# First block's attention on one core: scores in two rounded passes over stacked keys, masks and maxima in rounded operands

## The reference, cut to what matters

```python
def window_attention(q, k, v, kc, vc, sink):
    ...
    s_loc = jnp.einsum('bnqkgd,bnjkd->bnkgqj', qb, kw).astype(jnp.float32) * scale
    s_ctx = jnp.einsum('bnqkgd,bckd->bnkgqc', qb, kc).astype(jnp.float32) * scale
    ...
    valid = (kpos >= 0) & (kpos < s) & (jnp.abs(qpos - kpos) <= WINDOW)
    s_loc = jnp.where(valid[None, :, None, None], s_loc, -jnp.inf)
    ...
    p = jax.nn.softmax(jnp.concatenate([s_loc, s_ctx, sl], axis=-1), axis=-1)

def global_attention(q, k, v, kc, vc):
    ...
    kall = jnp.concatenate([k, kc], axis=1)
    ...
    o = lax.map(lambda qblk: gqa_attend(qblk, kall, vall), qb)
```

## Time and profile before

| what | value |
|---|---|
| median of 3 runs | 3219.28 us (3214.47 to 3220.64) |
| the profiled execution, span from first to last instruction | 3215.5 us (its own time is not listed apart) |
| PE busy | 2983.4 us, 93% of the span |
| PE weight loads | 1880.8 us, 58% |
| DVE busy | 1100.8 us, 34% |
| ACT busy | 737.7 us, 23% |
| POOL busy | 381.7 us, 12% |
| mean granted clock of PE | 0.961 |
| first attention, 281.33 to 450.81 us | 169.5 us |
| second attention, 1272.23 to 1397.71 us | 125.5 us |

### The profile page before, as it was taken

One profiled execution on the slowest core, in us unless ns is written; L12 is line 12 of the kernel. 1 busy time (PEld: TensorE's weight loads), 2 busy tenths in 40 slices (PEclk: granted clock), 3 DMA queues, 4 the chain that ended last, 5 costly groups with the idle time before them and its releaser, 6 DMA issues.

```text
span 3215.5 us, 50344 instructions
## 1 busy us (share of the span) xinstructions
PE 2983.4 (93%) x21802; PEld 1880.8 (58%) x21802; DVE 1100.8 (34%) x1930; ACT 737.7 (23%) x1393; POOL 381.7 (12%) x494
## 2 busy tenths in 40 slices
PE   6999989699999998986988888999999999999999
PEld 3645556455555464554433333888865568678887
DVE  4124754211111244643222224322434463232242
ACT  3113651000000133541000002222322362222232
POOL 2022520122222121411000000000000000000000
PEclk8998989799999999997999999999999989999999
DMA  8930033899999810037999996122311202231130
GB/s 342 394 129 1 1 144 120 344 401 409 408 409 408 308 55 1 1 138 290 417 423 423 424 423 252 59 105 79 113 67 55 69 18 79 79 111 65 66 140 30
DMA packets 138400, 626.97 MB, mean 195 GB/s; under 512 B 12592, under 2 KB 19776, under 8 KB 82896
## 3 DMA queue, kind: packets, MB, share of 16 engines
q1 hardware_dynamic: 122064, 577.67, 44.8%
q0 software_dynamic: 16128, 46.18, 4.3%
HBM read 607.36 MB, written 16.45 MB: 194 GB/s over the span
## 4 chain that ended last, share of the span: by engine, by line
PE 42%; DMA 10%; DVE 2%; ACT 1%; issue 1%; SPq 0%; POOL 0%; DVEq 0%; ACTq 0%; POOLq 0%
PE bank L959 19%; DMA slots<-in_w_up_dram 10%; PE bank L1526 7%; PE bank L1714 4%; PE bank L1403 3%; PE bank L1630 3%; PE bank L1283 1%; PE bank L1647 1%; PE bank L1424 1%; PE bank L1658 0%; PE bank L1453 0%; PE bank L1648 0%; SPq L910 0%; PE bank L1060 0%; PE bank L1061 0%
## 5 line engine op out<-in xcount | busy, mean ns | idle before, releaser
L1403 PE MATMUL bank<-slots,HT 128*32 128x256 f32 x8192 | 478.0, 383 | 52.4 <-DMA slots<-in_w_gate_dram 24.2
L1403 PEld LDWEIGHTS bank<-slots,HT 128*32 128x32 f32 x8192 | 265.6, 111 | 269.0 <-issue 62.6
L959 PE MATMUL bank<-hT_high,chunk_high 128*128 128x512 f32 (+2 forms) x736 | 285.1, 387 | 5.3 <-DVE hT_low L2500 5.3
L959 PE MATMUL bank<-hT_high,low_slots 128*128 128x512 f32 (+2 forms) x736 | 287.1, 390 | 0.0
L959 PE MATMUL bank<-hT_low,chunk_high 128*128 128x512 f32 (+2 forms) x736 | 285.5, 388 | 0.0
L2091 ACT ACTIVATE arena<-bank 128x512 f32<-128x512 f32 x32 | 19.1, 597 | 756.2 <-PE bank L1403 433.8
L959 PE MATMUL bank<-slots,HT 128*128 128x512 f32 (+4 forms) x544 | 180.3, 491 | 7.2 <-issue 5.8
L2843 DVE TENSOR_TENSOR arena<-bank,arena 128x512 f32<-128x512 f32 x32 | 22.1, 692 | 441.9 <-ACT arena L2091 441.9
L959 PEld LDWEIGHTS bank<-hT_high,chunk_high 128*128 128x128 f32 x736 | 139.0, 189 | 35.7 <-DVE hT_low L2500 5.7
L959 PEld LDWEIGHTS bank<-hT_low,chunk_high 128*128 128x128 f32 x736 | 138.8, 189 | 32.4 <-issue 0.2
L959 PEld LDWEIGHTS bank<-hT_high,low_slots 128*128 128x128 f32 x736 | 138.7, 188 | 29.7
(11 more groups left out here) (453 smaller groups left out, 4897.4 us busy)
## 6 DMA issues: line engine op xcount, KB each, us to landing
slots<-in_w_gate_dram SPq DMA_DIRECT2D x128, 1024.0 KB, 19.5
slots<-in_w_up_dram SPq DMA_DIRECT2D x128, 1024.0 KB, 21.7
arena<-in_w_down_dram SPq DMA_DIRECT2D x80, 1024.0 KB, 23.3
arena<-in_ada_w_dram SPq DMA_DIRECT2D x48, 1024.0 KB, 9.1
X<-in_w_down_dram SPq DMA_DIRECT2D x32, 1024.0 KB, 18.3
slots<-in_w_in_dram SPq DMA_DIRECT2D x15, 2048.0 KB, 8.9
slots<-in_ffn_w_gate_dram SPq DMA_DIRECT2D x10, 2048.0 KB, 8.5
slots<-in_ffn_w_up_dram SPq DMA_DIRECT2D x10, 2048.0 KB, 8.9
```

Of the source, the lines that this page charges most:

```text
L959: mm = pe.matmul(out_, lhsT, rhs, start=(n == 0), stop=(n == len(pairs) - 1))
L1403: mm = pe.matmul(bank[32 * j:32 * j + 32, 2 + n, 256 * g:256 * g + 256], xT[:, 64 * k + 32 * g:64 * k + 32 * g + 32], columns(w[:, c, :], ...
```

## The change

It does the following, in both layers unless said.

- Keys are split into a rounded part and the rest. ACT rounds them into `k_high` (64 rows and the row of ones); DVE subtracts, writes the rest into partitions 64 to 127 of `k_both`, and copies the rounded part into partitions 0 to 63 (`stack_keys`). `k_both` lies on the place of `K_ext`.
- Queries are rounded by ACT into partitions 0 to 63 and once more into 64 to 127 of `q_twice` (for the first layer's context queries `q_twice_ctx`, which lies on the context tiles of `X`). POOL subtracts and keeps the rest of the queries in `q_low`, on the place of `Q_ext` (`query_rest`); row 64 there holds the negated maxima.
- A score product is `k_both` times `q_twice` over 128 rows, plus `k_high` times `q_low` over 65 rows: two rounded matmuls in place of a plain one.
- Row scores lose row 64, and the context groups' go through rounded operands too. The maxima that are subtracted are rounded (`neg_max`).
- The mask products use `mask_ident` and `mask_band`, rounded once by ACT in the first layer's `qkv`; the two copies that `latent_in` made of them go.
- ACT rounds the third and fourth main group at steps 1 and 3 of group 0; before, at step 1 of the first two main groups.
- The two context tiles of `X` are loaded in `conv_out` and no longer in `qkv`; POOL's memset of row 64 of the queries goes.

```diff
-        k_round = [rounded(f"k_round{l}", slots_at, unit % SLOTS * SLOT, 2, 2, NTOK) for l, unit in enumerate(first_slots("qkv"))]
-        q_round = [rounded(f"q_round{l}", slots_at, (unit + 1) % SLOTS * SLOT, 2, HEADS, SEQ)
+        k_high = [rounded(f"k_high{l}", slots_at, unit % SLOTS * SLOT, 2, 2, NTOK) for l, unit in enumerate(first_slots("qkv"))]
+        k_both = rounded("k_both", arena_at, at_moe, 2, 2, NTOK)
+        q_twice = [rounded(f"q_twice{l}", slots_at, (unit + 1) % SLOTS * SLOT, 2, HEADS, SEQ)
                    for l, unit in enumerate(first_slots("qkv"))]
+        q_twice_ctx = rounded("q_twice_ctx", X_at, ST * D, 2, HEADS, CTX)
+        q_low = [rounded(f"q_low{l}", slots_at, unit % SLOTS * SLOT, 2, HEADS, NTOK) for l, unit in enumerate(first_slots("w_out"))]
...
+        neg_max = nc.alloc_sbuf_tensor_at("neg_max", [P, 16], F32R, offset=neg_max_at)
...
+        mask_ident = nc.alloc_sbuf_tensor_at("mask_ident", [P, P], F32R, offset=mask_ident_at)
+        mask_band = nc.alloc_sbuf_tensor_at("mask_band", [P, 2, P], F32R, offset=band_at)
...
-                        mains = sum(other.main for other in groups[:group.number + 1])
-                        pe.wait_ge(sem["rounded"], st.at("rounded", 2 * mains))
+                        pe.wait_ge(sem["rounded"], st.at("rounded", (4 if st.layer == 0 else 3) * mains_to(group) - 1))
...
-                    kT = K_ext[0:HD + 1, group.kind, group.g, :]
+                    kT = k_high[st.layer][0:HD, group.kind, group.g, :]
                     if not group.main:
                         for j in range(2):
-                            mm = pe.matmul(bank[:, b, CTX * j:CTX * j + CTX], q_ext[0:HD + 1, group.kind, group.heads + j, tile_cols(qt)],
+                            mm = pe.matmul(bank[:, b, CTX * j:CTX * j + CTX],
+                                           q_twice_ctx[0:HD, group.kind, group.heads + j, tile_cols(qt - ST)],
                                            kT[:, SEQ:NTOK], start=True, stop=True)
                         mm.then_inc(sem["rowmax_full"], 1)
                         return
-                    kT = k_round[st.layer][0:HD + 1, group.kind, group.g, :]
-                    q = q_round[st.layer][0:HD + 1, group.kind, group.heads + unit.j, tile_cols(qt)]
...
                         pe.wait_ge(sem["shift_done"], st.at("shift_done", group.number + 1))
-                    keys = K_ext[0:HD + 1, group.kind, group.g, tile_cols(one.kt)]
+                        for name in ("rows_high", "rows_split") if group.main else ():
+                            pe.wait_ge(sem[name], st.at(name, mains_to(group)))
+                    both = k_both[:, group.kind, group.g, tile_cols(one.kt)]
+                    high = k_high[st.layer][0:HD + 1, group.kind, group.g, tile_cols(one.kt)]
+                    rest = q_low[st.layer][0:HD + 1, group.kind, :, :]
                     for j, b, event, previous in one.parts:
                         if previous is not None:
                             pe.wait_ge(sem["prob_ready"], st.at("prob_ready", previous + 1))
                         if j is None:
-                            pe.matmul(bank[:, b, :].rearrange("p (a n) -> p a n", a=2), keys,
-                                      q_ext[0:HD + 1, group.kind, group.heads:group.heads + 2, SEQ:NTOK],
-                                      start=True, stop=True).then_inc(sem["score_full"], 1)
+                            out_ = bank[:, b, :].rearrange("p (a n) -> p a n", a=2)
+                            pe.matmul(out_, both, q_twice_ctx[:, group.kind, group.heads:group.heads + 2, :], start=True, stop=False)
+                            pe.matmul(out_, high, rest[:, group.heads:group.heads + 2, SEQ:NTOK],
+                                      start=False, stop=True).then_inc(sem["score_full"], 1)
                             continue
                         edges = []
                         if group.kind == 0 and one.kt < ST:
                             edges = [(t, 0 if t < one.kt else 1) for t in (one.kt - 1, one.kt + 1) if 0 <= t < ST]
-                        mm = pe.matmul(bank[:, b, 0:one.hi - one.lo], keys, q_ext[0:HD + 1, group.kind, group.heads + j, one.lo:one.hi],
-                                       start=True, stop=not edges)
+                        pe.matmul(bank[:, b, 0:one.hi - one.lo], both, q_twice[st.layer][:, group.kind, group.heads + j, one.lo:one.hi],
+                                  start=True, stop=False)
+                        mm = pe.matmul(bank[:, b, 0:one.hi - one.lo], high, rest[:, group.heads + j, one.lo:one.hi],
+                                       start=False, stop=not edges)
                         for t, side in edges:
                             lo = P * t - one.lo
-                            mm = pe.matmul(bank[:, b, lo:lo + P], ident[:, :], band[:, side, :], start=False, stop=t == edges[-1][0])
+                            mm = pe.matmul(bank[:, b, lo:lo + P], mask_ident[:, :], mask_band[:, side, :], start=False, stop=t == edges[-1][0])
                         mm.then_inc(sem["score_full"], 1)
 
...
-                    act.activation(q_ext[HD:HD + 1, group.kind, group.heads:group.heads + 2, group.queries[0]:group.queries[1]],
+                    act.activation(q_low[st.layer][HD:HD + 1, group.kind, group.heads:group.heads + 2, group.queries[0]:group.queries[1]],
                                    bank[0:1, 4:6, 0:n], ACT.Copy).then_inc(sem["shift_done"], 1)
 
                 def round_operands(group):
 
                     kind, g = group.kind, group.g
-                    act.activation(k_round[st.layer][0:HD + 1, kind, g, :], K_ext[0:HD + 1, kind, g, :], ACT.Copy)                       .then_inc(sem["rounded"], 1)
-                    act.activation(q_round[st.layer][0:HD + 1, kind, 2 * g:2 * g + 2, :], q_ext[0:HD + 1, kind, 2 * g:2 * g + 2, 0:SEQ],
-                                   ACT.Copy).then_inc(sem["rounded"], 1)
+                    heads = q_ext[0:HD, kind, 2 * g:2 * g + 2, :]
+                    q = q_twice[st.layer][:, kind, 2 * g:2 * g + 2, :]
+                    q_ctx = q_twice_ctx[:, kind, 2 * g:2 * g + 2, :]
+                    act.activation(k_high[st.layer][0:HD + 1, kind, g, :], K_ext[0:HD + 1, kind, g, :], ACT.Copy).then_inc(sem["rounded"], 1)
+                    act.activation(q[0:HD], heads[:, :, 0:SEQ], ACT.Copy).then_inc(sem["rounded"], 1)
+                    if st.layer == 0:
+                        act.activation(q_ctx[0:HD], heads[:, :, SEQ:NTOK], ACT.Copy).then_inc(sem["rounded"], 1)
+                    doubled = act.activation(q[HD:P], heads[:, :, 0:SEQ], ACT.Copy)
+                    if st.layer == 0:
+                        doubled = act.activation(q_ctx[HD:P], heads[:, :, SEQ:NTOK], ACT.Copy)
+                    doubled.then_inc(sem["rounded"], 1)
...
-                        if n == 1 and to_round and group.main:
+                        if n in (1, 3) and to_round:
                             round_operands(to_round.pop(0))
...
+                def stack_keys(group):
+
+                    mains = sum(other.main for other in groups[:group.number + 1])
+                    dve.wait_ge(sem["rounded"], st.at("rounded", (4 if l == 0 else 3) * (mains - 1) + 1))
+                    keys, high, both = [v[:, group.kind, group.g, :] for v in (K_ext, k_high[l], k_both)]
+                    step(dve.tensor_tensor(both[HD:P], keys[0:HD], high[0:HD].bitcast(F32), ALU.subtract))
+                    dve.tensor_copy(both[0:HD], high[0:HD].bitcast(F32)).then_inc(sem["rows_high"], 1)
 
...
+                    if group.main:
+                        stack_keys(group)
                     for unit in group.units:
                         maximum(unit)
                 for group in groups:
                     units = groups[group.number + ahead].units if group.number + ahead < len(groups) else []
+                    if units and units[0].group.main:
+                        stack_keys(units[0].group)
                     for unit in units:
                         maximum(unit)
...
+                def query_rest(number):
+
+                    kind, heads = mains[number].kind, slice(mains[number].heads, mains[number].heads + 2)
+                    pool.wait_ge(sem["rounded"], st.at("rounded", (4 if l == 0 else 3) * (number + 1)))
+                    rest, whole = q_low[l][0:HD, kind, heads, :], Q_ext(l)[0:HD, kind, heads, :]
+                    ins = pool.tensor_tensor(rest[:, :, 0:SEQ], whole[:, :, 0:SEQ], q_twice[l][0:HD, kind, heads, :].bitcast(F32), ALU.subtract)
+                    if l == 0:
+                        ins = pool.tensor_tensor(rest[:, :, SEQ:NTOK], whole[:, :, SEQ:NTOK], q_twice_ctx[0:HD, kind, heads, :].bitcast(F32),
+                                                 ALU.subtract)
+                    ins.then_inc(sem["rows_split"], 1)
+
+                query_rest(0)
                 for part, (lo, hi) in enumerate(parts):
```

(8 more changed lines are left out.)

32 lines of the change are left out of this document (19 added, 13 removed).

## The result

The changed kernel took **3249.91 us** (median of 4 runs, 3241.33 to 3271.55), the kernel before 3217.07 in the runs beside it: a ratio of 1.011, 95% interval 1.0082 to 1.0138. It is 33 us slower, and 40 above the range's upper end. The profiled execution took 3257.27 us, with a span of 3255.4.

The account below looks back on a forecast made before the run. PE was taken to bound only cold and PE-bound pieces, with DVE and ACT holding the relays around group changes. First attention −14.2, second −14.3, loads +1 gave −27.5 us against the median 3219.28: 3192 us, range 3177 to 3210.

Parts of the forecast that it names:

- What PE gets back: Both attentions: PE work saved on scores, row scores and masks, 54.6 us at 2.4 GHz, a bound from above when warm.
- A score matmul becomes two rounded passes: Score products in both attentions: two rounded passes instead of four, so half of each matmul's time goes.
- 96 fewer mask records: Sign expected in the changed profile: mask products keep one record of two, so 96 go.
- The masks' 10.3 us saving: Mask products on PE: 96 records of 128 columns go, at about 0.107 us each, 10.3 us.
- POOL's first tap: First attention, group 0: ready at about 325 to 328 us, ACT stalls before its fifth tap, +3.5 us.
- the stacking: Key stacking ahead of DVE's maximum: +1.5 at 323 to 341, +0.7 at 358 to 379, +1.5 at 1337 to 1349.
- Rival (d): Both attentions: a less busy engine is granted 1.2 GHz longer; 60 us more there gives 33 slower, 3252 us; chance 0.05.
- Rival (b): Both attentions: relays hold nearly everything, only three PE-bound pieces give (12.3 us); gain 5, 3214 us; chance 0.15.
- Rival (c): Taps in group 0: DVE and POOL block each other wholly, 8 us worse, 3204 us; chance 0.10.
- third to a half: Overlap of DVE and POOL: priced as a slowing by this much, not as one blocking the other wholly.
- The loads at +1: Two x loads moved behind attention, ahead of six others on POOL's queue: later landing priced +1 us, between 0 and 2.5.
- the signs named as wrong: An attention over 20 us shorter, POOL's tap before ACT asks for the fifth, or cold stretches over 27.1 and 22.7 us.

Follow-up runs that it names:

- e8: The kernel before with sequence scores in two rounded passes and rounded masks, remainders left out, row scores over 65 partitions: 3194.05 us, ratio 0.992.
- e9: e5 without the remainders: DVE's key stacking left out, POOL's subtractions replaced by a zero fill, first score pass on the rounded keys: 3189.33 us, ratio 0.9923.
- e5: The changed kernel with its row-score matmuls over 65 partitions again instead of 64: 3222.94 us, ratio 1.0014.
- e7: The kernel before with its row-score matmuls of sequence queries over 64 partitions instead of 65: 3241.04 us, ratio 1.0072.
- e12: e5 without DVE's key stacking, so the keys' remainders stay out of the scores; POOL's query subtractions kept: 3202.79 us, ratio 0.9964.
- e13: e5 with POOL's query subtractions replaced by a zero fill, DVE's key stacking kept: 3202.86 us, ratio 0.997.
- e2: The kernel before with sequence score matmuls as two rounded passes instead of four, remainders left out, no work added on other engines: 3187.98 us, ratio 0.9907.
- e10: e8 with one rounded pass for each sequence score instead of two: 3184.21 us, ratio 0.9898.
- e1: The changed kernel with the first of its two rounded score passes issued three times, giving PE its old score load: 3256.9 us, ratio 1.0128.

## Why the prediction was wrong

The stages' way from 309.4 to 357.9 us, in measured steps: PE's passes and masks −27.6 (e8); ACT's further roundings, a fill on POOL, the later start and the rounded context scores +4.4 (e9); the remainders +30.3 (e5); 64 partitions +41.4. By the ratios of the whole times the same four are −26, +1, +29 and +31.

- **"What PE gets back"** was sound: 54.6 us at 2.4 GHz as a bound. e8 leaves the context queries as they were (3.4 + 5.1 of it), so 46 us of work went, PE's busy time fell by 36.8 and the stages by 27.6. "A score matmul becomes two rounded passes" and "96 fewer mask records" came true.
- **The step that failed** is one that isn't in the sum: the row scores went from 65 to 64 partitions and I priced that at nothing, without a sentence. It cost 41 us in the traces (31 by whole times): 29 (23) as gaps alone, as e7 has them at an unchanged clock, and the rest with the remainders around, where the changed kernel has 55 us more at 1.2 GHz than e5. The rest is near the scatter, and how it splits into waits and clock is open. The masks' 10.3 us saving turned into a loss by the price of 0.16 us: the 48 row masks now have a gap on either side, an estimated 15 us; the 48 masks of the score products stand beside 65 partitions and have none.
- **Mis-sized:** the side work. The sum had terms of 3.5 for POOL's first tap, 1.5 and 0.7 for the stacking in the first attention and 1.5 in the second, about 7 in all; the remainders cost 30. Each place was right: PE waited 4.5 us for the first roundings (4.0 before), the tap came at 327.01 us (predicted 325 to 328), ACT waited for it, `stack_keys` stood ahead of the maximum. But PE waited 7.7 us, not 3.5, and the stacking took up to 3.4 us beside POOL, not 1.5 to 1.9. Of the 30 us between e9 and e5, 19.8 are idle time of PE and 10.5 busy time, with 30 us more at 1.2 GHz. In the traces the larger part comes only when both parts are there, with 27 to 30 us of cold time (e5 against e12, e13), but the whole times have 13 and 15 us for each alone; which it is stays open.
- **Rival (d)**, slower by the clock, gave 3252, near the result, and for the most part for a wrong reason. Its premise, an engine with less to do, fails in e2 and e8, which keep the clock (69 and 77 us cold against 74). Its size was near: 104 us more at 1.2 GHz hold at most 52 us of full-clock work, where (d) had 60. But the clock fell with the gaps and the waits together; e7 has the gaps and e12 and e13 one source of waits each, and they have 73, 93 and 96 us cold against 178. Where exactly the grant turns stays open.
- **Rival (b)**, the relays hold, shows in e10, where PE idles for most of what it is spared. Rival (c), DVE and POOL blocking each other: stacking beside POOL took 3.4 us against 1.5 alone. The subtraction and the copy each took 0.95 us longer, twice and 2.7 times their time, beside POOL operations of 1.0 to 1.8 us. That is nearer to the whole blocking of (c) than to the "third to a half" that I took, but it was not tried by itself.
- The loads at +1: the stages behind the first attention up to the end of the output projection took 109.1 us before and 109.5 after.
- Of the signs named as wrong one did show: three cold stretches of 31 us, against 27.1 and 22.7, and 103 and 75 us cold in all. The other two did not: no attention got shorter, and POOL's first tap did not come early.

## What to carry to other kernels

Compare the partition counts of neighbouring matmuls, not only their passes and columns. A contraction over 64 partitions between ones over 65 or 128 cost 0.16 us at each change here, more than the 128-column pass it stood beside; a 65th row that adds a harmless constant took it away. When remainders or copies are put on engines that already pass work to each other around a change of group, measure them together as well as one by one: here they cost 29 to 30 us where their terms were put at 7. And thin what stands ahead of the awaited operation (here taps) before giving up precision.

## What the runs showed that I had not expected

- A rounded 128-column pass is followed after 0.11 us, or after 0.25 where the neighbour changes between 64 and 128 partitions; the load of weights isn't longer for it (0.18 us at 64 partitions, 0.19 at 65).
- A window of 31 us with PE busy in all of it ran wholly at 1.2 GHz (345 to 376 us), behind waits and among such gaps. e1, with the same gaps but twice the score passes (39 us more of PE's work at full clock), had 105 us cold in the two stages where the changed kernel had 178, and they were 5 us shorter. By whole times the two can't be told apart.
- DVE's subtraction of 64x768 took 0.95 us alone and 1.91 beside POOL, its copy 0.55 and 1.50.
